# Moving the split sources of a two-block transformer kernel's wide projections by 64 bytes against the weights

## The reference

```python
y = hybrid_mixer(x, ...)                    # ends in merged @ w_out
x = layer_norm(ALPHA * x + y, ...)
y = mem_cross_attention(x, mem, ...)        # ends in o @ w_o
x = layer_norm(ALPHA * x + y, ...)
y = (silu(g) * u) @ w_out                   # [256, 5632] @ [5632, 2048]
...
x = x + gate1 * (mix @ w_out)
x = x + gate2 * ((silu(a) * v) @ w_down)    # [256, 5632] @ [5632, 2048]
```

## The kernel before

| tensors | before | modulo 256 | after | modulo 256 |
|---|---|---|---|---|
| whi, wlo | 49280, 65664 | 128, 128 | the same | 128, 128 |
| xhi, xlo | 82112, 98752 | 192, 192 | the same | 192, 192 |
| ohi, olo, ckhi, cklo, merged, mixT | 134336 and up | 192 | the same | 192 |
| shi, slo | 82048, 86144 | 128, 128 | 83008, 87104 | 64, 64 |
| hid | 134272 | 128 | 134208 | 64 |
| dhi | 179328 | 128 | 179264 | 64 |
| dlo1, dlo2 | 187520, 213120 | 128, 128 | 187456, 213056 | 64, 64 |
| silu | 183424 | 128 | 183360 | 64 |
| gate_row | 90304 (in xhi) | 192 | 106944 (in xlo) | 192 |
| small, expo | 133728, 133696 | 96, 64 | 133696, 228928 | 64, 64 |

## Time and profile before

### The profile page before, as it was taken

How to read it: one execution, slowest core, us unless ns; L and a number is a source line. 1 busy time by engine, 2 the same in 40 slices (tenths; PEclk the granted TensorE clock), 3 DMA queues, 4 the chain that set the end, 5 groups by cost and what they waited for, 6 DMA issues and landing times.

```text
span 2691.7 us, 46200 instructions
## 1 busy us (share of the span) xinstructions
PE 2588.6 (96%) x18094; PEld 2416.8 (90%) x18094; DVE 1649.6 (61%) x1911; ACT 1253.4 (47%) x1513; POOL 87.1 (3%) x141
## 2 busy tenths in 40 slices
PE   7999999999889999999999979999899999999997
PEld 7979999999779999999988868978799999997885
DVE  3555466456758777767777764555656565655555
ACT  3454465444454444444444454434445555554443
POOL 0000000000101000000000010000000000000000
PEclk9999999999999999999999989999899999999998
DMA  7445534557646888888877725425355555555552
GB/s 272 175 154 195 184 138 156 188 216 280 253 157 266 313 335 314 336 311 336 338 291 293 277 110 188 156 95 187 125 175 186 186 187 187 187 187 187 187 197 99
DMA packets 79993, 579.04 MB, mean 215 GB/s; under 512 B 8880, under 2 KB 9008, under 8 KB 9776
## 3 DMA queue, kind: packets, MB, share of 16 engines
q1 hardware_dynamic: 64208, 465.60, 47.0%
q0 software_dynamic: 14000, 101.46, 9.8%
q10 hardware_dynamic: 1712, 10.95, 1.1%
HBM read 575.87 MB, written 2.10 MB: 215 GB/s over the span
## 4 chain that ended last, share of the span: by engine, by line
PE 95%; DVE 2%; issue 1%; POOL 1%; ACT 1%; DMA 0%; DVEq 0%; ACTq 0%; POOLq 0%; SPq 0%
PE ps L1449 59%; PE ps L1488 25%; PE ps L1453 7%; POOL small L401 1%; PE ps L1686 0%; DVE res L1118 0%; PE ps L1422 0%; DMA mem_nat<-in_mem 0%; DVE xlo L886 0%; DVE xn L1147 0%; PE ps L1549 0%; PE ps L1720 0%; PE ps L1752 0%; PE ps L1731 0%; PE ps L1582 0%
## 5 line engine op out<-in xcount | busy, mean ns | idle before, releaser
L867 DVE TENSOR_TENSOR wlo<-raw,whi 128x1024 fp32r<-128x1024 f32 x876 | 1059.0, 1224 | 824.1 <-ACT whi L478 819.4
L478 ACT ACTIVATE whi<-raw 128x1024 fp32r<-128x1024 f32 x876 | 917.3, 1060 | 1072.2 <-PE ps L1449 646.9
L1449 PE MATMUL ps<-xhi,whi 128*128 128x256 f32 x4240 | 1191.1, 281 | 17.1 <-DVE wlo L867 8.2
L1449 PE MATMUL ps<-xhi,wlo 128*128 128x256 f32 x4240 | 1188.4, 280 | 0.0
L1449 PE MATMUL ps<-xlo,whi 128*128 128x256 f32 x4240 | 1187.7, 280 | 0.0
L1449 PEld LDWEIGHTS ps<-xhi,whi 128*128 128x128 f32 x4240 | 798.8, 188 | 18.8 <-issue 11.6
L1449 PEld LDWEIGHTS ps<-xlo,whi 128*128 128x128 f32 x4240 | 800.1, 189 | 0.4
L1449 PEld LDWEIGHTS ps<-xhi,wlo 128*128 128x128 f32 x4240 | 798.7, 188 | 0.0
L1488 PE MATMUL ps<-whi,dhi 128*128 128x512 f32 x704 | 217.7, 391 | 4.1 <-DVE conv L1368 4.1
L893 DVE SCALAR_TENSOR_TENSOR ada<-ada,cb 128x2048 f32<-128x2048 f32 x96 | 219.3, 2285 | 0.0
L1488 PE MATMUL ps<-wlo,dhi 128*128 128x512 f32 x704 | 217.7, 390 | 0.0
(11 more groups left out here) (256 smaller groups left out, 1771.7 us busy)
## 6 DMA issues: line engine op xcount, KB each, us to landing
raw<-in_stream SPq DMA_DIRECT2D x438, 1024.0 KB, 4.8
ada<-in_w_ada POOLq DMA_DIRECT2D x96, 1024.0 KB, 6.7
gamma<-in_ln_g ACTq DMA_DIRECT2D x3, 1024.0 KB, 7.0
beta<-in_ln_b ACTq DMA_DIRECT2D x3, 1024.0 KB, 11.0
mem_nat<-in_mem SPq DMA_DIRECT2D x2, 1024.0 KB, 7.6
res<-in_x SPq DMA_DIRECT2D x1, 2048.0 KB, 21.4
res<-in_x ACTq DMA_DIRECT2D x1, 2048.0 KB, 9.8
out<-xn SPq DMA_DIRECT2D x4, 512.0 KB, 2.7
```

The source lines that it names most:

```text
L478: act.activation(whi[:, h % 4], raw[g % 4][:, 1024 * half:1024 * half + 1024], ACT.Copy)\
L867: dve.tensor_tensor(wlo[:, h % 4], raw[g % 4][:, 1024 * half:1024 * half + 1024], whi[:, h % 4].bitcast(F32), ALU.subtract).then_inc(lo_re ...
L1449: ins = pe.matmul(o, w[:, k, P * m:P * m + P], a[:, kt], start=begins and n == 0 and m % 2 == 0, stop=ends and n == 2, skip_group_check=True)
```

## The change

It edits the layout alone. A new base `at_hid` is the address 64 bytes under the weights' base, modulo 1024; `at_pool` lies 128 above it, where it was. The sources of the down projections, hid, dhi, dlo1 and dlo2, and the buffer silu are counted from at_hid, 64 bytes lower than before. shi and slo move to 64 bytes below the weights' base modulo 1024, which is 960 bytes up. Since slo then ends inside the place that gate_row had in xhi, gate_row moves to the same place in xlo, and expo moves behind mod, so that at_pool stays.

```diff
-        expo = sb("expo", [P, 4])
         small = sb("small", [P, 128])
-        at_pool = place[0] + SHIFT + (at_shi - place[0]) % 1024
+        at_hid = place[0] + (at_shi - SHIFT - place[0]) % 1024
+        at_pool = at_hid + 2 * SHIFT
         at_pool2 = at_pool + 49152
 
-        shi = sb("shi", [P, 4, S], F32R, at_shi)
-        slo = sb("slo", [P, 4, S], F32R, at_shi + 4096)
-        gate_row = sb("gate_row", [P, D], F32, at_xhi + 8192)
+        shi = sb("shi", [P, 4, S], F32R, at_shi + 1024 - SHIFT)
+        slo = sb("slo", [P, 4, S], F32R, at_shi + 1024 - SHIFT + 4096)
+        gate_row = sb("gate_row", [P, D], F32, at_xlo + 8192)
...
         mod = sb("mod", [P, ADA])
+        expo = sb("expo", [P, 4])
...
-        hid = sb("hid", [P, FT, S], F32, at_pool - SHIFT)
-        dhi = sb("dhi", [P, 4, S], F32R, at_pool + 45056 - SHIFT)
-        dlo = [sb("dlo1", [P, 4, S], F32R, at_pool2 + 4096 - SHIFT), sb("dlo2", [P, 4, S], F32R, at_pool2 + 28672 + 1024 - SHIFT)]
-        silu = sb("silu", [P, 1024], F32, at_pool2 - SHIFT)
+        hid = sb("hid", [P, FT, S], F32, at_hid)
+        dhi = sb("dhi", [P, 4, S], F32R, at_hid + 45056)
+        dlo = [sb("dlo1", [P, 4, S], F32R, at_hid + 49152 + 4096), sb("dlo2", [P, 4, S], F32R, at_hid + 49152 + 28672 + 1024)]
+        silu = sb("silu", [P, 1024], F32, at_hid + 49152)
```

## The result

The changed kernel takes 2702.10 us, the median of eight executions (2695.37 to 2706.12); the kernel before, also in eight, 2694.32 us. The ratio is 1.0027, with a 95% interval of 1.0017 to 1.0037, or 5 to 10 us more. (Ratios here are estimates with intervals of their own and not exactly the quotients of the medians.) The forecast was 2686.0 us, 6.7 less than the 2692.74 us that it started from. The time lies inside the stated range and the direction is wrong.

What follows compares the result with a forecast made beforehand. TensorE was taken as the bound, the wide matmuls' pitch setting a wide stage's cost. One term, 6.7 us less, took the span from 2691.7 to 2685.0 us and the median to 2686.0 us; range 2671 to 2703 us.

Steps and rivals of the forecast that it cites:

- What bounds the kernel: TensorE holds 95% of the chain; L1488's 2976 wide matmuls at a pitch of 226.7 ns take 674.7 us, 25%.
- Only the wide loop changes its relation: All 2976 matmuls of L1488 go from stationary level with moving to stationary 64 bytes below; no other matmul changes.
- the rest of the edit: Moves of hid, silu, expo, small and gate_row, with VectorE, ScalarE and DMA effects, were costed at nothing.
- The relation matters: At 336 and 512 columns, stationary above moving is dearer than level, by 3 and 6.6 ns.
- The price: At L1488, 64 below saves 2.25 ns a matmul, read from 256-column matmuls at L1449; x 2976 = 6.7 us less.
- the other way: Bound for L1488 if only distance counts: 6.6 ns more, 19.7 us; by the 336-column difference of 3.3 ns, 9.9 us.
- rival B: Wide matmuls: each 64 bytes downward takes 6.6 ns; pitch 220.1 ns, 2673.0 us; chance 0.20.
- Rival C: Wide matmuls: level and below cost the same, or address counts for nothing; 226.7 ns, 2692.7 us; chance 0.26.
- Rival D: Every L1488 matmul slower by 3.3 to 6.6 ns, distance counting, not direction; 2702.6 to 2712.4 us; chance 0.21.
- The signs of being wrong: Mechanism wrong if a piece outside L1488 moves over 1 us, or the wide pitch splits by operand (shi against dhi).

Runs made afterwards that it cites:

- h1: The kernel before with every tensor 64 bytes higher, all relations between tensors kept; 2693.49 us, ratio 1.0005.
- h2: The changed kernel with every tensor 64 bytes higher, wide sources still 64 below the weights; 2700.08 us, ratio 1.0034.
- both half changes: The changed kernel with only shi and slo 64 below the weights: 2694.75 us; with only the down projections' sources (and silu) 64 lower: 2697.67 us.
- g3: The kernel before with one extra 64-column matmul after each of the 22 chunks of up1; 2696.73 us, 3.1 more.

## Why the prediction was wrong, by its steps

**What bounds the kernel: right.** TensorE's pitch at L1488 is the cost of a wide stage. The down1 piece moved by 2.32 us with its count unchanged, and no wait took any of it.

**Only the wide loop changes its relation: right**, and the rest of the edit was worth nothing, as costed: with shi and slo back in their places, out1 took 85.96 us again though gate_row and expo stayed moved.

**The relation matters: right.** The slices of the earlier trace rows had leaned that way, by 2 to 3 ns, and h1 and h2 show that it is the relation.

**The price: this step failed.** I wrote "I take the T-form's value, 6.7 us less", and reasoned that if moving reads stall in the T-form, "the same stalls fall into a load that runs beside 512 columns". They do not. The N-form and the wide loop, both with 512 moving columns, take the same pitches at all eight relations, to 0.1 ns and but for a second pattern at 128, with different orders of loads and banks. The T-form, with 256, follows another law: level, their best relation, is one of its worst (120.0 ns). The right term is +2.2 ns (228.9 - 226.7) for 2880 matmuls and +6.7 for o_mem's 96, 6.3 + 0.6 = 6.9 us more (the five pieces show 6.75), in place of -2.25 ns and 6.7 us less. The bound "the other way" of +3.3 to +6.6 ns missed it as well, being too far out for most stages.

**The trend (rival B): refuted.** From above to level the pitch fell by 6.7 ns (233.3 to 226.7), from level to below it rose by 2.2.

**Rival C** leaned on the 336-column slices, which had level and 64 below alike. That holds for neither 256 nor 512 columns. The rule of the Trainium skill ("SBUF — State Buffer", section "SBUF: two separate sides") that PE never waits on anyone would have given no change at all. Here eight relations span 7.6 ns of pitch at 512 columns (226.7 to 234.3), so for the two operands of one matmul stream the measurement decides against it.

**Rival D had the sign and the place, with the wrong mechanism.** It said that distance alone counts, with a repeat of 128 bytes. But 64 above is 233.3 and 64 below 228.9, and 128 (232.4) is not the level value. That it came within its own threshold (a pitch over 228.5 ns), by 0.4 ns, is luck. So is the time's place inside the range: its upper end was set by this rival's lower price, 3.3 ns, from the 336-column slices.

**The signs of being wrong.** Both that the prediction named came up. Pieces outside L1488 moved by more than 1 us (gates, q_mem), and the wide pitch did not move as one, though it split by stage (o_mem at 233.3 ns) and not by operand. The first has nothing to do with the change: gates takes 181.17 us in both half changes and 181.16 in the changed kernel 64 bytes higher, as in the kernel before. Both come in the main from patterns that the prediction did not know of.

What stays open is why the relation costs what it does and what picks a pattern: no run shows where the lost nanoseconds arise.

## What to carry to other kernels

Read the price of a layout from matmuls of the same number of moving columns: here a value from 256 columns had the wrong sign at 512. Before a layout is moved for one loop, a single run that puts different relations into different stages reads several values of the law at once, though one short stage in one execution may show only one of two patterns. The level relation was the best for 512 columns, by 2.2 to 7.6 ns. A change of 0.3% in the median can be masked in any one profile by another stage, so compare the pieces of the chain and not the spans.

## What was not expected of the hardware

- **Two patterns.** With all addresses equal, a stretch of T-form matmuls runs at 117.8 or at 113.3 ns, mostly to its end. The gates stage did both, 181.17 and 174.35 us for its 1536 matmuls. Both traces show a wait of 1.6 us for VectorE at its start, and the two differ from the third matmul on.
- **A hiccup can change the pattern.** In the changed kernel 64 bytes higher, the stage of 432 matmuls before the N-form ran at 113.3 ns up to one distance of 0.22 us, and at 117.8 after it:

```profile
1616.82 0.28 PE L1450 MATMUL ps<-xhi,wlo 128*128 128x256 f32 x1
...
1617.95 0.38 PE L1450 MATMUL ps<-xhi,whi 128*128 128x256 f32 x1
1618.17 0.28 PE L1450 MATMUL ps<-xlo,whi 128*128 128x256 f32 x1
...
1619.94 0.28 PE L1450 MATMUL ps<-xlo,whi 128*128 128x256 f32 x1
```

Ten distances take 1.13 us before it and fifteen 1.77 us after it. In three more traces a stretch went from 113.3 to 117.8 at such a distance, with the same tensors read (up1 of the changed kernel, after its first 48 matmuls, is one). The extra matmul of g3 met only stretches that were already at 117.8.
- The patterns may be much of the spread between executions. The kernel before, run beside h1 and h2, took between 2669.10 and 2695.96 us in 31 executions. up2 and gates both at 113.3 ns would be 3840 x 4.45 + 6.8 = 24 us less, which would give that lowest time; no trace caught it, so this is an estimate.
- **Mixed relations are dearer than either.** 64 below for the high part and level for the low one took 230.0 ns, where all below took 228.9 in most stages and all level 226.7.
